# A split-float32 output projection: its first weight unit split one feature tile at a time, and unread products on TensorE ahead of it

## The reference, cut to what matters

```python
    h = h + jnp.concatenate([o_sb, o_rw], axis=-1) @ w_out[l]        # first block: 512x1024 @ 1024x1024
    xn = rmsnorm(h, norm_ffn_g[l]).reshape(B * S, D)
    y = hier_moe(xn, router_grp_w[l], ...)                           # top-1 group, top-2 experts in it
...
    merged = gates[:, :, 0] * br_a + gates[:, :, 1] * br_b
    x = x + merged @ w_out[layer]                                    # second block: 512x1024 @ 1024x1024
```

## Time and profile before

| | |
|---|---|
| the profiled execution's own time | 1426.43 us |
| its span, first to last instruction | 1424.6 us |
| median of the three runs | 1428.4 us |
| TensorE busy | 1279.5 us, 90% of the span |
| VectorE, ScalarE, GpSimd busy | 568.5, 478.3, 139.4 us |
| mean granted TensorE clock | 0.950 |
| first projection's products | 406.5 to 464.1 us |
| experts | about 489 to 745 us |
| second projection's products | 1371.9 to 1420.5 us |

### The profile page before, as it was taken

How to read it: one execution, slowest core, us unless ns; L and a number is a source line. 1 busy time by engine, 2 the same in 40 slices (tenths; PEclk the granted TensorE clock), 3 DMA queues, 4 the chain that set the end, 5 groups by cost and what they waited for, 6 DMA issues and landing times. The chain is left out here.

```text
span 1424.6 us, 24358 instructions
## 1 busy us (share of the span) xinstructions
PE 1279.5 (90%) x10299; PEld 991.4 (70%) x10299; DVE 568.5 (40%) x1026; ACT 478.3 (34%) x807; POOL 139.4 (10%) x202
## 2 busy tenths in 40 slices
PE   6999989999869499978863999999989979899988
PEld 5786855899658355544433988888967868666668
DVE  3335543556451332222226223444457745422232
ACT  4233557330343211101114334555455524111130
POOL 4000023000010123222110011222100000000000
PEclk9999999999979699989985999999999989999989
DMA  4422000000166599999964436222161145013021
GB/s 149 126 89 89 1 1 0 11 4 4 61 240 238 197 356 394 377 394 395 402 248 181 119 119 133 89 89 89 30 90 60 39 179 170 30 59 118 0 73 47
DMA packets 92488, 195.53 MB, mean 137 GB/s; under 512 B 9510, under 2 KB 73084, under 8 KB 79452
## 3 DMA queue, kind: packets, MB, share of 16 engines
q1 hardware_dynamic: 86604, 183.48, 37.7%
q0 software_dynamic: 5200, 8.40, 1.8%
q10 hardware_dynamic: 576, 2.10, 0.4%
HBM read 184.74 MB, written 16.81 MB: 141 GB/s over the span
## 5 line engine op out<-in xcount | busy, mean ns | idle before, releaser
L1825 PE MATMUL hidden_ps<-w_gate,gathered_t 128*64 128x256 f32 x432 | 113.9, 424 | 23.5 <-DMA w_up<-exp_w_up_dram 22.7
L1825 PE MATMUL hidden_ps<-w_up,gathered_t 128*64 128x256 f32 x432 | 114.0, 424 | 0.0
L1825 PEld LDWEIGHTS hidden_ps<-w_gate,gathered_t 128*64 128x64 f32 x432 | 63.7, 153 | 60.6 <-issue 32.0
L641 DVE TENSOR_TENSOR w_in_low<-w_in_raw,w_in_high 128x2048 fp32r<-128x2048 f32 x20 | 45.8, 2292 | 116.4 <-ACT w_in_high L633 116.4
L1388 PE MATMUL wo_ps<-w_out_high,wo_x_high 128*128 128x256 f32 x256 | 75.9, 296 | 16.6 <-DVE w_out_low L641 16.6
L593 PE MATMUL proj_ps<-block_in_high,w_in_low 128*128 128x512 f32 x232 | 90.7, 391 | 0.0
L593 PE MATMUL proj_ps<-block_in_low,w_in_high 128*128 128x512 f32 x232 | 90.6, 391 | 0.0
L593 PE MATMUL proj_ps<-block_in_high,w_in_high 128*128 128x512 f32 x232 | 90.5, 390 | 0.0
L593 PE MATMUL gate_ps<-block_in_high,gate_w_high 128*128 128x512 f32 x192 | 80.0, 417 | 11.3 <-DVE gate_w_low L641 11.3
L593 PE MATMUL gate_ps<-block_in_low,gate_w_high 128*128 128x512 f32 x192 | 76.5, 398 | 0.0
L593 PE MATMUL gate_ps<-block_in_high,gate_w_low 128*128 128x512 f32 x192 | 76.4, 398 | 0.0
(11 more groups left out here) (457 smaller groups left out, 3101.3 us busy)
## 6 DMA issues: line engine op xcount, KB each, us to landing
w_gate<-exp_w_gate_dram SPq DMA_DIRECT2D x27, 1024.0 KB, 24.5
w_up<-exp_w_up_dram SPq DMA_DIRECT2D x27, 1024.0 KB, 28.9
w_down<-exp_w_down_dram SPq DMA_DIRECT2D x27, 1024.0 KB, 29.1
w_in_raw<-w_in_dram SPq DMA_DIRECT2D x20, 1024.0 KB, 5.6
slot_scratch_and_keys<-w_in_dram SPq DMA_DIRECT2D x14, 1024.0 KB, 5.3
vb<-w_in_dram SPq DMA_DIRECT2D x6, 1024.0 KB, 5.5
gate_w_raw_odd<-w_in_dram SPq DMA_DIRECT2D x6, 1024.0 KB, 5.9
slot_scratch_and_keys<-exp_w_gate_dram SPq DMA_DIRECT2D x5, 1024.0 KB, 26.8
```

The source lines that it names most:

```text
L641: dve.tensor_tensor(self.part[1][n % 2], self.slot(n), self.part[0][n % 2], ALU.subtract).then_inc(self.low, 1)
L1825: x = pe.matmul(g_bank[e % 2][a * CAP:(a + 1) * CAP, 0:DE], xT[e % 2][:, k, :], w[:, k, :], start=(k == 0), stop=(k == KC - 1))
```

## The change

`SplitWeights` gets `first_high` and `first_low`, which split one feature tile (128x256) of unit 0. In `out_projection`, ACT and DVE alternate between an operand's feature tile and the same feature tile of weight unit 0, and TensorE waits for both for each feature tile. The counts `wts.high` and `wts.low`, on which everything else waits, are raised once after the eighth. `keep_busy` issues plain float32 products of `heads` with itself, 128x128 each, into a PSUM bank where nobody reads them: ten at the end of TensorE's part of `rwkv_output`, six at the start of TensorE's part of `out_projection` when it is called with `early`. Both projections get the new splitting; only the first gets the extra products.

```diff
+def keep_busy(pe, const, out, n):
+    for _ in range(n):
+        pe.matmul(out[:, 0:P], const["heads"][:, :], const["heads"][:, :], start=True, stop=True)
...
+    def first_high(self, act, k, made):
+        if k == 0:
+            act.wait_ge(self.loaded[0], 16)
+        act.activation(self.part[0][0][:, k, :], self.raw[0][:, k, :], ACT.Copy).then_inc(made, 1)
+
+    def first_low(self, dve, k, high, made):
+        dve.wait_ge(high, k + 1)
+        dve.tensor_tensor(self.part[1][0][:, k, :], self.raw[0][:, k, :], self.part[0][0][:, k, :], ALU.subtract).then_inc(made, 1)
...
                         pe.matmul(v_bank[i % 2][:, :], const["heads"][:, :], sq[:, i % 2, :], start=True, stop=True).then_inc(var, 1)
+                keep_busy(pe, const, o_bank[0], 10)
...
             def _(pe):
+                if head:
+                    keep_busy(pe, const, banks[5], 6)
                 for u in range(NU):
-                    wts.wait(pe, u)
+                    if u:
+                        wts.wait(pe, u)
                     for k in range(KC):
                         if u == 0:
+                            pe.wait_ge(w_low, k + 1)
                             pe.wait_ge(x_low, k + 1)
...
                 for k in range(KC):
                     act.activation(x[0][k], xT[:, k, :], ACT.Copy).then_inc(x_high, 1)
-                    if k == 0:
-                        wts.split_high(act, 0)
+                    wts.first_high(act, k, w_high)
+                act.sem_inc(wts.high)
                 wts.split_high(act, 1)
...
                     dve.tensor_tensor(x[1][k], xT[:, k, :], x[0][k], ALU.subtract).then_inc(x_low, 1)
-                    if k == 0:
-                        wts.split_low(dve, 0)
+                    wts.first_low(dve, k, w_high, w_low)
+                dve.wait_ge(w_low, KC)
+                dve.sem_inc(wts.low)
```

More of the change, by code:

```diff
@@ L1338, in out_projection @@
         x_high, x_low, ready, added, stored = (s.sem(f"{tag}_{n}") for n in ("x_high", "x_low", "ready", "added", "stored"))
+        w_high, w_low = s.sem(f"{tag}_first_w_high"), s.sem(f"{tag}_first_w_low")
         wts.used = lambda n: (ready, TT * (n + 1))
```

## The result

The changed kernel takes 1416.78 us (median of four, 1413.71 to 1417.15); the kernel before, with one more run, 1427.44. The ratio is 0.9922, interval 0.9909 to 0.9935. The forecast, 1420.0 of 1427.4, is a ratio of 0.9948: right in direction, too small in size, with the measured time near the low end of the range. The profiled execution takes 1416.70 us, its span 1414.9.

What follows compares the result with a forecast made beforehand. It took the kernel as bound by TensorE's late start in each output projection, then slow at the low clock. Gains of 4.3 (first) and 3.0 (second) sum to 7.3 us: 1420.0 from 1427.4, range 1416.5 to 1424.4.

Steps and rivals of the forecast that it cites:

- Earlier start: First projection: with weight unit 0 sliced, TensorE's first product can start 3.0 us earlier, at 403.45 instead of 406.48.
- First projection's clock: Three cases for TensorE's clock with the unread products, gaining 5.4, 4.3 or 2.5 us in the first projection; 4.3 taken.
- case (b): First projection: clock falls between the unread batches, rises 3.0 to 3.4 us after 401.6; gain 4.3 us; taken, chance 0.60.
- case (a): First projection: the hole between the unread batches doesn't lower the clock; gain 5.4 us there, 8.4 in all; chance 0.12.
- What waits on the counter: First projection: with wts.low rising later, weight unit 2 still lands near 418; no cost, 1.5 us or so cover.
- ACT's queue turns on TensorE: Rival, first projection: weight unit 2 lands at 428.8, TensorE stands 9.2 us; 1.6 us slower, 1429.0; chance 0.03.
- Second projection: First product at 1368.86 instead of 1371.89: 3.0 us taken; 1.2 us more if the clock returns sooner, not counted.
- luck at the restarts: 1.5 us either way for the clock's level at later restarts; used in the range's fast end, 1416.4.
- Does it reach the end: Router, gather and experts pass on all of the first projection's 4.3 us, with 1.5 us either way.
- The base: Forecast made from 1427.4, the mean of four times of the kernel before, 1426.3 to 1428.4.

Runs made afterwards that it cites:

- again: The change as a whole, unchanged and run again; 0.9934 of the kernel before.
- again_late: The change with about 1.5 us of VectorE steps (one memset, three multiplications) added to the router's chain ahead of the experts; 0.9930 of the kernel before.
- same_late: The kernel before with one memset and five multiplications on VectorE added to the router's chain, 2.4 us meant; 0.9994 of the kernel before.
- split_2: Repeat of the change with both keep_busy calls taken out, so splitting by feature tile alone; 0.9966 of the kernel before.
- split: The change with both keep_busy calls taken out, so splitting by feature tile alone; 0.9975 of the kernel before.
- busy: The kernel before with keep_busy and its two calls put in, weight unit 0 still split whole; 0.9974 of the kernel before.
- busy_2: Repeat of the kernel before with keep_busy and its two calls put in, weight unit 0 still split whole; 0.9968 of the kernel before.
- same: The kernel before, unchanged and run again; 1.0005 of the kernel before.
- same_2: The kernel before, unchanged, its third profile; 1.0013 of the kernel before.
- split_six: The change without the ten unread products, keeping the splitting and the six; 0.9951 of the kernel before.

## Why the prediction was right and where it was wrong

**Earlier start: right.** 3.0 us forecast for each projection, 3.07 measured. The slice took 0.41 us alone and 0.33 in sequence, a pair every 0.93 to 0.94 us on DVE (400.58, 401.52, 402.45), as worked out. Eight slices of 0.33 us cost DVE 0.3 us more than the 2.29 us of the whole unit, behind TensorE's start, where nobody waited. What the Trainium skill ("VectorE: DVE Perf Modes", "The TRN2 errata — SBUF-src ops pay a fixed extra latency per instruction") says of small tiles agrees with this: eight slices cost DVE more than one whole unit. It did not matter here.

**First projection's clock: right as cases, wrong as to which is worth what.** From ACT's first split to the start of DVE's last addition of unit 0 it took 18.85 us before (401.67 to 420.52), 14.4 in again (case b, gain 4.45 forecast 4.3) and 13.4 in the change's first profile (case a, gain 5.4 forecast 5.4). But the extra of case (a) was given back within unit 1, so both gain 4.1 us at the projection's end. The chances were off as well: of the ten profiles with the sliced start and both batches, three are case (a), which had 0.12, and seven case (b).

**What waits on the counter: wrong.** "Lands near 418 again ... cost nothing, with 1.5 us or so of cover left." Unit 2 landed 18.0 us after ACT's first split where it had landed 16.3 after it, and in case (a) unit 0 ended about 1 us earlier than in the case on which I reckoned the cover (13.4 us after ACT's first split in place of 14.4). The rival "ACT's queue turns on TensorE" was thus the true mechanism at a small size: 1.1 us, in one case of two. A landing 18.0 us after ACT's first split is 419.7 on the time scale of the kernel before, and from 419.6 on the rival was to decide. (That rival's sum takes off 7.6 us where its terms, 4.3 and 3.0, make 7.3; nothing else used it.)

**Second projection: sized too small.** I took 3.0 us; 54.2 went to 50.0 three times and 51.1 once, so 3.1 to 4.2. The term that was missed is the clock, whose gain I had named (1.2 us) and left out: it was low for 3.4 us of TensorE's run (1364.6 to 1368.0) where it had been low for 5.9 (1371.89 to 1377.8), and that run is 1.1 us shorter.

**Together** the two own stretches went from 117.15 us (mean of three profiles of the kernel before) to 109.16 (four of the change): 8.0 us, against 7.3 forecast. The times differ by more: the change's four ratios, 0.9922 to 0.9934, are 9.4 to 11.1 us. That the measured time still lies inside the range, 0.3 us from its end, is partly luck: that end was built from case (a) gaining 5.4 us in the first projection and luck at the restarts, and neither projection's term nor the rest came out that way.

**Does it reach the end: this step failed.** "I take all of it, with 1.5 us either way." This took the rest of the kernel to be the same on average but for luck. More than all arrived: 1.2 to 3.1 us beyond the own stretches in the change's four runs. The experts' stretch is 241.2 us on average before (239.1, 242.2, 242.3) and 239.7 in the change (239.4 to 239.9). Across all 20 profiles it goes with how late the clock returns: 239.1 to 240.9 where it is back within 3.9 us of the first product, 241.5 to 244.9 where it takes 4.4 or more. On average that makes 1.5 us between the two kernels. That the moment of the start decides it is borne out by one run (again_late) and missed by two (same_late and split_2), so it isn't shown. What lies ahead of ACT's first split and between the experts and the second projection differs by another 3 us between the profiles of the two kernels, but is the same code (apart from the ten products, which end before DVE does) and spread over 2.7 and 5.9 us among all profiles.

The rest can be set beside what each run changed. The timed gain less the gain of the run's own two stretches is -2.6 and -1.5 us for split and split_2, and between +0.9 and +4.0 us for each of the other runs whose first projection has unread products, busy (+2.6) and busy_2 (+3.8) among them. same, same_2 and same_late give -2.0 to +1.1. Each figure sets the time of all executions beside the stretches of one profile, with an interval of about 2 us or more either way, but the mean is +2.4 over the fourteen runs with unread products and -1.1 over the five without. So unread products seem to go with a gain outside the stretches that they stand in. The profiles point the same way, though they spread widely: with the ten products the experts' stretch is 240.1 us on average, without them 241.6, and the stretch behind the experts 633.2 against 635.0. How some products near 394 us could do that wasn't traced; the cause stays open, and with it that of the part of the gain that the prediction had at nothing.

**The base.** The three runs shown before spread over 2 us; with more, one kernel spread from 1422 to 1434. A range worked out from 1426.3 to 1428.4 was too trusting of three runs.

## What to carry to other kernels

Where a stage starts with two operands to be prepared, prepare them in the order and the pieces in which they are used; the gain is the whole of what was prepared too early, and it can be read off the timeline beforehand to a tenth of a microsecond. Test each batch of products that is meant to keep TensorE's clock up by itself and in its own stretch: here either batch alone brought nothing there, both together 1.1 us. Read a change by its own stretches in several profiles before believing a difference of a few microseconds in the whole, and look who shares a queue with each counter that now rises later.

## What was not expected of the hardware

- The clock can stay at its upper level over a hole of 3.2 us on TensorE and fall 1.3 us into the work that follows (busy: hole from 401.1 to 404.3, fall at 405.6); in the change's second projection too it fell 1.3 us after the products had begun (1363.30, 1364.6), behind a hole of 3.8 us. So TensorE was slow in a stretch in which it was busy throughout.
- With unchanged code, one and the same start of the experts finds the clock back after 2.3 or after 5.4 us (before, same). In the profile of same (first product at 494.3, last at 736.2):

```profile
L1825 PE MATMUL hidden_ps<-w_gate,gathered_t x432: 379/379/687, 494.3 to 736.2; 128*64 128x256 f32 x144
```

```profile
499.00:500.00 1.00, 1.00 (x8) 0.61 (x6) 0.00 (x0) 0.00 (x0) 0.00 (x0) 0.63 0.00 0
```

- The late return is not all that this costs. In the profile of same the clock falls a second time, from 503.2 to 506.6 us, while TensorE is busy; in that of before it stays up from 497.2 us on past 590. This stretch of same:

```profile
503.20:506.60 3.40, 3.40 (x18) 1.96 (x16) 0.56 (x1) 0.00 (x0) 0.93 (x1) 0.50 1.01 429
```

- Together the clock is low for 39.5 us within the experts' stretch of same and for 33.1 within that of before. At half pace the 6.4 us more are 3.2 us of work, and the stretches differ by 3.1 us (242.2 and 239.1). The second fall is in five profiles, those in which the clock returned 5.1 us or more after the first product, and comes 8.5 to 8.9 us after that product (same, same_2, split, split_six, again_late). They are low for 39 to 43 us in all and take 241.8 to 244.9 us. The fifteen others are low for 30 to 35 us and take 239.1 to 241.6.
